# Expert weight loads of an MoE layer split by partition: 120 rows in one DMA, 8 rows in another

## The chip, the cores and the metric

The kernel runs on one core of one Trainium2 chip. The metric is the device time of one launch in microseconds (us); lower is better. A core has TensorE (matmuls), VectorE, ScalarE, GpSimd, and SyncE, which here issues nearly all DMAs, and 16 DMA engines that move the data of all of them. On-chip memory has 128 partitions.

## The reference

A trunk of two layers with 640 tokens (128 context, 512 latent) of width 1024. Each layer mixes tokens (attention and two kinds of scans), and then mixes channels by an expert-choice mixture of 16 experts. The change concerns the second half, of which this is the core:

```python
cap = EC_FACTOR * (bsz * n_tok) // N_EXPERTS
aff = jax.nn.softmax((xf @ router).astype(jnp.float32), axis=-1)
gate, idx = lax.top_k(aff.T, cap)
xe = xf[idx]
he = jax.nn.silu(jnp.einsum('ecd,edf->ecf', xe, w1)) * jnp.einsum('ecd,edf->ecf', xe, w3)
ye = jnp.einsum('ecf,efd->ecd', he, w2) * gate[..., None].astype(h.dtype)
y = jnp.zeros_like(xf).at[idx.reshape(-1)].add(ye.reshape(-1, dm))
```

Each expert takes 80 tokens (64 latent, 16 context) and has three matrices of 1024 × 1024 in float32: 12.6 MB an expert, 201 MB a layer. Everything is float32.

## The kernel before

The program is a list of phases for each of the two layers: modulation, input projection, attention, the two scans, output projection and norm, routing, experts, second norm. Each phase writes out the instruction stream of every engine by hand; order between engines is kept by semaphores, and there is no scheduler.

In the expert phase an expert is cut into four *quarters* (q = 4 x + j for expert x, quarter j). For a quarter of the hidden width, `gate(x, j)` (line 2285) runs 128 matmuls with w1 and w3 as the stationary side (64 in the source; each stands as two in the trace) and 80 tokens as the moving side; for a quarter of the output width, `project(x, j)` (line 2300) runs 64 with w2, one expert later. ScalarE applies silu (line 2390), VectorE multiplies (line 2470) and takes the projections out of PSUM (line 2430). Every two experts, TensorE turns the results (line 2311) and adds them to their tokens by a matmul with a selection matrix (lines 2329 and 2338); VectorE adds these to the residual (line 2439). GpSimd gathers the tokens of the expert after next (line 2044).

The weights come by SyncE. `load_w13` (line 2055) loads a gate quarter, 128 partitions × 4096 float32, 2 MB, into one of WG = 6 buffers; `load_w2` (line 2061) loads a projection quarter, 128 × 2048, 1 MB, into one of WP = 4. In the input each partition's row of a quarter is contiguous: 16 KB and 8 KB. Each buffer has its own semaphore (`ld_e0` to `ld_e5`, `ld_f0` to `ld_f3`), which a load raises by 16 when all of it has landed. Five gate quarters are issued in the output phase, ahead of the stores of the normalised rows to memory (line 1967); the sixth and four projection quarters in the routing phase (behind the router's weights, ahead of the context lists, line 2099). In the expert phase SyncE then goes through the quarters: it waits until gate(q) has run and loads quarter q + 6 into its buffer, waits until project(q − 4) has run and loads w2 of quarter q. The last buffers that come free take the next layer's modulation weights (line 393, five loads of 2 MB).

TensorE waits for a quarter's semaphore ahead of its first matmul (`gate_loads` gives the count), for the product of two quarters before, and within a quarter for nothing.

Of the kernel before, what the change touches and what calls it, by code (L numbers as in the profile page):

```python
# [25 lines left out]
P = 128  # L26
# [14 lines left out]
NE, FF = 16, 1024  # L41
# [1956 lines left out]


WG, WP = 6, 4  # L2000
QUARTERS = 4 * NE
FREED_GATES = QUARTERS - WG

# [5 lines left out]

def gate_loads(l, q):  # L2010

    return 16 * (l * len(range(q % WG, QUARTERS, WG)) + q // WG + 1)


def expert_memory(e):
# [36 lines left out]

def load_w13(e, sp, q, mem):

    sp.dma_start(mem["w13"][q % WG].rearrange("p a k n -> p (a k n)"), e.d["ex_w13"][e.l, q // 4, q % 4].rearrange("p a k n -> p (a k n)")
                 ).then_inc(e.S[f"ld_e{q % WG}"], 16)


def load_w2(e, sp, q, mem):

    sp.dma_start(mem["w2"][:, q % WP].rearrange("p k n -> p (k n)"), e.d["ex_w2"][e.l, q // 4, q % 4].rearrange("p k n -> p (k n)")
                 ).then_inc(e.S[f"ld_f{q % WP}"], 16)


ROUTE_SEMS = (
# [135 lines left out]
def phase_experts(e):  # L2201

    nc, d, l, S, ps, x_sb = e.nc, e.d, e.l, e.S, e.ps, e.x
    mem = expert_memory(e)
    w13, w2, xe, xT, hs, he, yS, yX, yP, yC, GP, GC, iP, gP, iC, gC, iota = (mem[k] for k in (
        "w13", "w2", "xe", "xT", "hs", "he", "yS", "yX", "yP", "yC", "GP", "GC", "iP", "gP", "iC", "gC", "iota"))
# [22 lines left out]
    with nc.Block() as block:  # L2229
        @block.sync  # L2230
        def _(sp):
# [5 lines left out]
            for q in range(QUARTERS):  # L2237
                if q + WG < QUARTERS:
                    sp.wait_ge(S["h_ps"], q + 1)
# [20 lines left out]
        def _(pe):  # L2260
# [29 lines left out]
            def project(x, j):  # L2290

                q = 4 * x + j
                pe.wait_ge(S[f"ld_f{q % WP}"], l * (16 * NE) + (x * 16 + 16))
                pe.wait_ge(S["he"], 4 * x + 4)
                if q >= 2:
                    pe.wait_ge(S["pr_sb"], q - 1)
                for b in range(2):
                    for f in range(KD):
                        for c in range(2):
                            m = nc.tensor.matmul(product(j)[c * 64:(c + 1) * 64, b, :],  # L2300
                                                 w2[:, q % WP, f, b * P + c * 64:b * P + (c + 1) * 64],
                                                 he[:, x % 2, f, :], start=f == 0, stop=f == KD - 1)
                m.then_inc(S["pr_ps"], 1)
# [297 lines left out]
```

## Time and profile before

| | us |
|---|---|
| median of 3 runs | 3454.83 (3450.43 to 3464.23) |
| the profiled execution's own time | 3457.51 |
| its span in the trace | 3455.7 |
| TensorE, matmuls busy | 2651.1 (77%) |
| TensorE, weight loads busy (beside the matmuls) | 2021.6 (58%) |
| VectorE / GpSimd / ScalarE busy | 1272.5 / 682.6 / 475.0 |
| 16 DMA engines, mean rate over the span | 154 GB/s |

How to read it: times come from one profiled execution. Engines are PE (TensorE's matmuls), PEld (its weight loads, which overlap them), DVE (VectorE), ACT (ScalarE), POOL (GpSimd), SPq (SyncE's queue). L2285 is line 2285 of the kernel. A group's idle time is that of the engine just ahead of the group's instructions, and behind the arrow stands what ended it; "issue" means that the engine waited for nothing that the profile shows. The DMA share is the mean busy share of the 16 DMA engines; the profile doesn't name the engine that a packet used. The matmuls' ends are modelled and overlap the next start. Queue q1 holds the DMAs that SyncE issues, q8 transfers of the kind "instruction". Some matmul records can be missing.

The expert phases lie at about 1105 to 1730 us and 2805 to 3427 us of the span.

### The profile page before, as it was taken

What the parts mean: (1) busy time and instruction counts of PE and PEld (TensorE: products, weight loads), DVE (VectorE), ACT (ScalarE), POOL (GpSimd) and SP (SyncE); (2) the same over time, 40 slices, a digit from 0 to 9 for tenths busy, and PEclk for the clock granted to TensorE, in tenths of its full rate; (3) what the DMA queues carried; (4) which work ended last, traced back from release to release, by engine and by line L of the source; (5) the groups of instructions that cost most, each with busy time, mean ns of one, the idle gap of its engine ahead of it and who ended that gap; (6) DMA issues with size and microseconds to landing.
All of it is one profiled execution on the core that took longest, in us unless ns stands there. A gap on an engine that the chain in (4) does not pass through costs nothing. (4 is left out here: it accounts for less than half of the span.)

```text
span 3455.7 us, 87591 instructions
## 1 busy us (share of the span) xinstructions
PE 2651.1 (77%) x40000; PEld 2021.6 (58%) x40000; DVE 1272.5 (37%) x2847; ACT 475.0 (14%) x973; POOL 682.6 (20%) x844
## 2 busy tenths in 40 slices
PE   5998883748584888888979988566585858888886
PEld 1555553638534777777725545355484457777774
DVE  1101568784523112211240026786744231112114
ACT  0102332032101000000010023302211100000001
POOL 0000908334221000000010027272430200000001
PEclk9999997869886999999999999877798879999998
DMA  8300000000053988888671010000003458888872
GB/s 350 125 25 36 1 1 11 1 7 4 3 219 139 363 339 338 308 333 325 248 301 61 4 36 1 9 3 7 2 3 123 182 188 321 344 343 335 337 287 105
DMA packets 69616, 532.75 MB, mean 154 GB/s; under 512 B 13920, under 2 KB 15776, under 8 KB 32896
## 3 DMA queue, kind: packets, MB, share of 16 engines
q1 hardware_dynamic: 66176, 516.66, 38.4%
q0 software_dynamic: 3072, 10.49, 1.1%
q8 instruction: 316, 5.18, 0.6%
q14 instruction: 52, 0.43, 0.0%
HBM read 518.34 MB, written 8.79 MB: 153 GB/s over the span
## 5 line engine op out<-in xcount | busy, mean ns | idle before, releaser
L2285 PE MATMUL ps<-arena 128*64 128x80 f32 x16384 | 620.0, 235 | 107.3 <-issue 102.6
L2285 PEld LDWEIGHTS ps<-arena 128*64 128x64 f32 x16384 | 596.0, 139 | 130.0 <-issue 128.4
L2300 PE MATMUL ps<-arena 128*64 128x80 f32 x8192 | 324.2, 234 | 55.5 <-issue 53.8
L2300 PEld LDWEIGHTS ps<-arena 128*64 128x64 f32 x8192 | 304.0, 138 | 66.0 <-issue 65.7
L526 PE MATMUL ps<-arena 128*128 128x128 f32 (+1 forms) x1088 | 296.4, 435 | 5.3 <-DVE arena L579 5.3
L2470 DVE TENSOR_TENSOR arena<-arena,ps 128x160 f32<-128x160 f32 x128 | 41.2, 322 | 653.4 <-ACT arena L2390 653.4
L526 PEld LDWEIGHTS ps<-arena 128*128 128x128 f32 x1088 | 164.8, 192 | 137.0 <-issue 131.2
L2044 POOL DMA_INDIRECT arena<-h_d,arena x32 | 39.8, 1243 | 1025.9 <-DVEq L2411 920.9
L2390 ACT ACTIVATE arena<-ps 128x160 f32<-128x160 f32 x128 | 38.8, 303 | 1132.8 <-PE ps L2285 1132.8
L583 DVE COPY arena<-ps 128x128 f32<-128x128 f32 (+3 forms) x48 | 16.3, 341 | 399.4 <-PE ps L526 287.6
L1979 PE MATMUL ps<-arena 128*128 128x512 f32 x320 | 142.9, 610 | 25.1 <-DMA arena<-in_w_out 25.1
L2430 DVE TENSOR_TENSOR arena<-ps,modc 128x128 f32<-128x128 f32 (+1 forms) x256 | 49.8, 236 | 292.1 <-PE ps L2300 292.1
L2329 PE MATMUL ps<-arena 128*128 128x512 f32 x256 | 123.4, 615 | 15.4 <-DVE x_sb L2439 12.3
L1111 PE MATMUL ps<-arena 128*128 128x256 f32 x80 | 34.9, 527 | 127.1 <-DVEq L1207 127.1
L826 POOL COPY arena<-arena 32x896 f32<-32x896 f32 x2 | 1.8, 924 | 642.1 <-DVE arena L866 642.1
L428 PE MATMUL ps<-arena,scT 128*2 128x512 f32 x384 | 88.0, 614 | 49.5 <-DMA arena<-in_ada_w 24.6
L532 PE MATMUL ps<-arena 128*128 128x512 f32 (+2 forms) x480 | 125.4, 423 | 0.0
L1979 PEld LDWEIGHTS ps<-arena 128*128 128x128 f32 x320 | 62.5, 196 | 104.6 <-issue 78.7
L532 PEld LDWEIGHTS ps<-arena 128*128 128x128 f32 x480 | 82.0, 189 | 42.8 <-issue 38.5
L883 DVE TENSOR_REDUCE arena<-ps 128x1 f32<-128x768 f32 (+1 forms) x80 | 65.8, 823 | 100.3 <-PE ps L718 93.8
L2439 DVE TENSOR_TENSOR x_sb<-x_sb,ps 128x512 f32<-128x512 f32 x116 | 78.9, 687 | 36.6 <-PE ps L2329 33.9
L1111 PEld LDWEIGHTS ps<-arena 128*128 128x128 f32 x80 | 16.0, 249 | 129.3 <-DVEq L1207 128.7
(345 smaller groups left out, 4065.3 us busy)
## 6 DMA issues: line engine op xcount, KB each, us to landing
arena<-in_ex_w SPq DMA_DIRECT2D x128, 2048.0 KB, 9.1
arena<-in_ex_w SPq DMA_DIRECT2D x128, 1024.0 KB, 9.2
arena<-in_ada_w SPq DMA_DIRECT2D x24, 2048.0 KB, 15.5
arena<-in_w_t SPq DMA_DIRECT2D x34, 512.0 KB, 3.5
arena<-in_w_out SPq DMA_DIRECT2D x4, 2048.0 KB, 10.3
arena<-in_w_tok SPq DMA_DIRECT2D x2, 3712.0 KB, 16.9
h_d<-x_sb SPq DMA_DIRECT2D x10, 512.0 KB, 2.6
arena<-in_w_uq SPq DMA_DIRECT2D x2, 1536.0 KB, 6.5
```

The lines of the kernel that those rows point to most:

```text
L428: i = nc.tensor.matmul(ps[PAIR[c], s, :], e.scT[:, k, :], slots[(2 * s + c) % RING][:, k, :], start=k == 0, stop=k == KD - 1)
L526: i = nc.tensor.matmul(ps[:, n % 8, 0:c1 - c0], ring[:, a % WRING, k, :], e.hT[:, k, c0:c1], start=k == 0, stop=k == KD - 1)
L532: i = nc.tensor.matmul(ps[:, n % 8, 0:c1 - c0], e.hT[:, k, a * P:(a + 1) * P], tokw[:, k, c0:c1], start=k == 0, stop=k == KD - 1)
L883: v.link(nc.vector.reduce_max(negm[:, i:i + 1], sc[:, 0:c1 - c0], AX))
L1111: nc.tensor.matmul(two[:, :, 0:P], kT[:, 2 * dr + g // 2, cols], qz[:, g // 2, :, cols], start=True, stop=True)
L1979: m = nc.tensor.matmul(ps[:, 2 * (t % 4) + n, :], e.mixT[:, k, t * P:(t + 1) * P], wo[:, n, k, :], start=k == 0, stop=k == KD - 1)
L2285: m = nc.tensor.matmul(gated(j)[c * 64:(c + 1) * 64, f, a, :], w13[q % WG][:, a, k, f * P + c * 64:f * P + (c + 1) * 64], xT[:, x % 2, k, ...
L2300: m = nc.tensor.matmul(product(j)[c * 64:(c + 1) * 64, b, :], w2[:, q % WP, f, b * P + c * 64:b * P + (c + 1) * 64], he[:, x % 2, f, :], s ...
L2329: nc.tensor.matmul(ps[:, 6 + h, :], GP[:, (t - 1) * P:t * P], yP[:, h * 512:(h + 1) * 512], start=True, stop=True).then_inc(S["sp_ps"], 1)
L2430: m = nc.vector.tensor_tensor(to, product(j)[:, :, c0:c1], row, ALU.mult)
L2439: m = nc.vector.tensor_tensor(x_sb[:, t, half], x_sb[:, t, half], ps[:, 6 + h, :], ALU.add)
L2470: nc.vector.tensor_tensor(he[:, b, 2 * j:2 * j + 2, :], hs[:, j % 2], gated(j)[:, :, 1, :], ALU.mult).then_inc(S["he"], 1)
```

## The change

Every load of expert weights is issued as two DMAs, for partitions 0 to 119 and for partitions 120 to 127. Both raise the semaphore of the buffer by 16, so the counts that TensorE waits for are 32 per load in place of 16. The split is such that the 120 rows go over fifteen DMA engines (8 rows each) and the 8 rows over eight engines (one each); the sixteenth engine gets no expert weights. The bytes, the buffers, the places of the loads in SyncE's stream and all other loads are as before.

```diff
+PARTS = (slice(0, 120), slice(120, P))
...
-    return 16 * (l * len(range(q % WG, QUARTERS, WG)) + q // WG + 1)
+    return 32 * (l * len(range(q % WG, QUARTERS, WG)) + q // WG + 1)
...
-    sp.dma_start(mem["w13"][q % WG].rearrange("p a k n -> p (a k n)"), e.d["ex_w13"][e.l, q // 4, q % 4].rearrange("p a k n -> p (a k n)")
-                 ).then_inc(e.S[f"ld_e{q % WG}"], 16)
+    for part in PARTS:
+        sp.dma_start(mem["w13"][q % WG][part].rearrange("p a k n -> p (a k n)"),
+                     e.d["ex_w13"][e.l, q // 4, q % 4, part].rearrange("p a k n -> p (a k n)")
+                     ).then_inc(e.S[f"ld_e{q % WG}"], 16)
...
-    sp.dma_start(mem["w2"][:, q % WP].rearrange("p k n -> p (k n)"), e.d["ex_w2"][e.l, q // 4, q % 4].rearrange("p k n -> p (k n)")
-                 ).then_inc(e.S[f"ld_f{q % WP}"], 16)
+    for part in PARTS:
+        sp.dma_start(mem["w2"][part, q % WP].rearrange("p k n -> p (k n)"),
+                     e.d["ex_w2"][e.l, q // 4, q % 4, part].rearrange("p k n -> p (k n)")
+                     ).then_inc(e.S[f"ld_f{q % WP}"], 16)
...
-                pe.wait_ge(S[f"ld_f{q % WP}"], l * (16 * NE) + (x * 16 + 16))
+                pe.wait_ge(S[f"ld_f{q % WP}"], 32 * (l * NE + x + 1))
```

SyncE's stream at the start of the expert phase, before (`ctx_d` are the context lists, `in_ex_w` the expert weights; 4096 elements are a gate quarter's row, 2048 a projection quarter's):

```order
L2236 DMA arena<-ctx_d 128x1 x4
L2055 DMA arena<-in_ex_w 128x4096 x5
L2061 DMA arena<-in_ex_w 128x2048
L2055 DMA arena<-in_ex_w 128x4096
L2061 DMA arena<-in_ex_w 128x2048
```

The same place after the change (the first two of the five gate quarters, left out the rest, and the pair of a gate and a projection quarter that repeats from there):

```order
L2241 DMA arena<-ctx_d 128x1 x4
L2057 DMA arena<-in_ex_w 120x4096
L2057 DMA arena<-in_ex_w 8x4096
...
L2065 DMA arena<-in_ex_w 120x2048
L2065 DMA arena<-in_ex_w 8x2048
L2057 DMA arena<-in_ex_w 120x4096
L2057 DMA arena<-in_ex_w 8x4096
```

Each load has become a pair, the small part right behind the large one; the order of the quarters is the same.

SyncE's stream in the output phase, before (the norm's parameters, the first expert weights, the stores of the normalised rows):

```order
L1876 DMA arena<-in_ln_g 128x1024
L1876 DMA arena<-in_ln_b 128x1024
L2055 DMA arena<-in_ex_w 128x4096 x5
L1967 DMA h_d<-x_sb 128x1024 x5
L1953 UNCONDITIONAL_BRANCH
```

And after the change:

```order
L1876 DMA arena<-in_ln_b 128x1024
L2057 DMA arena<-in_ex_w 120x4096
L2057 DMA arena<-in_ex_w 8x4096
...
L1967 DMA h_d<-x_sb 128x1024 x5
L1953 UNCONDITIONAL_BRANCH
```

Ten issues stand ahead of the five stores in place of five. TensorE's stream has the same instructions in the same order; only the counts in its waits differ.

## Rows read from the trace of the kernel before

**Rows 1.** The page: busy time by engine, and the DMA queues (packets, MB, share).
```profile
PE 2651.1 (77%) x40000; PEld 2021.6 (58%) x40000; DVE 1272.5 (37%) x2847; ACT 475.0 (14%) x973; POOL 682.6 (20%) x844
...
q1 hardware_dynamic: 66176, 516.66, 38.4%
...
q8 instruction: 316, 5.18, 0.6%
```

**Rows 2.** The line of the gate matmuls in the first layer: duration, first and last start.
```profile
L2285 PE MATMUL ps<-arena x8192: 229/233/394, 1105.2 to 1702.0; 128*64 128x80 f32 x200
```

**Rows 3.** Timeline, end of the first expert stage: start, length, engine, line, operation, count.
```profile
1727.59 1.96 PE L2338 MATMUL ps<-arena 128*128 128x512 f32 x4
```

**Rows 4.** Windows: length, busy time (count) of each engine, granted clock, DMA share, GB/s.
```profile
core 0: us, PE busy (x) PEld busy (x) DVE busy (x) ACT busy (x) POOL busy (x), PEclk, DMA share, GB/s
...
789.00:815.00 26.00, 25.56 (x834) 25.56 (x836) 11.38 (x17) 5.37 (x9) 15.78 (x13) 0.94 0.02 4
1200.00:1600.00 400.00, 337.65 (x8066) 301.19 (x8065) 78.91 (x230) 18.74 (x52) 12.77 (x10) 1.00 0.86 332
2900.00:3300.00 400.00, 341.69 (x8142) 305.76 (x8140) 79.64 (x233) 19.87 (x54) 12.85 (x10) 0.99 0.86 335
20.00:60.00 40.00, 27.63 (x110) 5.25 (x112) 4.10 (x6) 0.00 (x0) 0.00 (x0) 0.91 1.02 420
```

**Rows 5.** Waits of SyncE's queue: waited for, us in total, times, longest us.
```profile
SPq L2055 <- PE ps L2285: 739.4, 116, 15.7
...
SPq L2061 <- PE ps L2300: 381.8, 120, 14.1
```

**Rows 6.** DMA issues by line: count, KB each, median us from issue to landing.
```profile
arena<-in_ex_w SPq DMA_DIRECT2D x128, 2048.0 KB, 9.1
arena<-in_ex_w SPq DMA_DIRECT2D x128, 1024.0 KB, 9.2
...
arena<-in_w_wa SPq DMA_DIRECT2D x4, 128.0 KB, 2.7
...
arena<-in_w_g SPq DMA_DIRECT2D x2, 128.0 KB, 2.6
```

**Rows 7.** Lines of TensorE, 1200 to 1600 us: count, busy us, mean ns, idle before.
```profile
L2285 PE MATMUL ps<-arena 128*64 128x80 f32 x5248 | 196.0, 233 | 36.6 <-issue 36.6
...
L2300 PE MATMUL ps<-arena 128*64 128x80 f32 x2603 | 102.8, 233 | 19.8 <-issue 18.1 <-DVE arena L2470 1.7
```

**Rows 8.** Waits of TensorE in the first expert stage.
```profile
PE ps L2285 <- issue: 51.7, 33, 2.9
PE ps L2300 <- issue: 27.6, 26, 2.5
```

**Rows 9.** Waits of TensorE in the second expert stage.
```profile
PE ps L2285 <- issue: 50.9, 29, 3.4
PE ps L2300 <- issue: 26.2, 23, 1.9
```

**Rows 10.** Timeline of TensorE in the first expert stage; in brackets idle before, us.
```profile
1145.23 0.91 PE L2300 MATMUL ps<-arena 128*64 128x80 f32 x20 [0.82 <-issue]
1146.07 0.77 PE L2269 MATMUL ps<-ident_sb,arena 80*128 80x80 f32 x8
1146.78 3.67 PE L2285 MATMUL ps<-arena 128*64 128x80 f32 x99
1152.30 1.25 PE L2285 MATMUL ps<-arena 128*64 128x80 f32 x29 [1.85 <-issue]
1153.33 2.44 PE L2300 MATMUL ps<-arena 128*64 128x80 f32 x64
1155.54 4.86 PE L2285 MATMUL ps<-arena 128*64 128x80 f32 x127
```

**Rows 11.** Timeline of TensorE where no large transfer runs.
```profile
796.31 1.10 PE L1598 MATMUL ps<-arena 64*64 64x64 f32 x32
797.25 1.10 PE L1614 MATMUL ps<-arena 64*64 64x64 f32 x32
```

**Rows 12.** Timeline of SyncE: the first loads issued in the first expert stage.
```profile
1111.97 10.59 SPq L2055 DMA_DIRECT2D arena<-in_ex_w  x3
```

**Rows 13.** The line of the gate loads: duration of an issue (min, median, max).
```profile
L2055 SPq DMA_DIRECT2D arena<-in_ex_w x128: 327/328/1470, 958.9 to 3348.6; - x128
```

## The prediction, made before the change was run

> **What bounds the kernel now.** I read the page's totals first, then the windows by stage, then the list of waits, then the timeline of the two places that matter. TensorE is the busiest engine, 2651.1 us of 3455.7 [rows 1]. The change touches only the loads of the expert weights, so only the two expert stages count: the first of them has its first gate matmul at 1105.2 and its last, short, matmuls of the scatter at 1727.59 [rows 2, 3]. Inside, TensorE is busy 337.65 us of 400 and the DMA engines have a mean share of 0.86 at 332 GB/s; in the second layer 341.69 us, 0.86 and 335 GB/s [rows 4]. So neither is full, and the question is what the idle time of TensorE is.
>
> It is no wait for weights. SyncE, which issues the loads, waits for TensorE to free a buffer in 116 of its waits for a gate quarter, 739.4 us, and in 120 for a projection quarter, 381.8 us [rows 5]: the loads follow the matmuls. A load lands 9.1 us (gate) or 9.2 us (projection) after its issue [rows 6], and a quarter takes about 400 / 41 = 9.8 us (5248 gate matmuls in 400 us, 128 to a quarter [rows 7]), while the buffers reach six gate quarters ahead. The weights are there long before.
>
> The idle time stands under "issue": nothing that the profile shows had to end. It is 51.7 + 27.6 us in the first layer [rows 8] and 50.9 + 26.2 us in the second [rows 9], **156.4 us** in all. The timeline tells its place: from 1145.23, where one stop ends, to the beginning of the next run 20 + 8 + 99 = 127 matmuls, and that next stop, the 1.85 us before 1152.30, falls in the middle of a gate quarter (99 of its matmuls ahead of it, 29 behind), where the code has no wait at all [rows 10]. One record is probably missing, so the distance is 128 matmuls, with their 128 weight loads 256 instructions. Queue q8, kind instruction, moved 5.18 MB in 316 packets, 16 KB each, beside 80,000 TensorE instructions in the page: 253 to a packet [rows 1]. So TensorE stops where its next block of instructions should have come. At 789 to 815 us the same fetches go on, faster: 32 matmuls in 0.93 us (from 796.31 to 797.25 [rows 11]), 128 in 3.7 us, and no stop is shown there, while the DMA engines have a share of 0.02 [rows 4]. **The fetches are late only when weights use the DMA engines.**
>
> [...]
>
> **The change part by part.** (1) *A sixteenth of the weights moves from one engine to eight others.* If the fetches run on the sixteenth, they wait behind no weights. The price of one stop is then what it is at 789 to 815: none. Bounds: 0 to 156.4 us over both layers. The five loads of the next layer's modulation weights at the end of the first stage still use all engines; of the 79.3 us a few stay. Per layer TensorE could gain about 75 us.
>
> (2) *Eight engines carry 9/8 of the rows.* This is the new limit. At 20 to 60 us the engines are full: 420 GB/s at a share of 1.02, so 26.3 GB/s each, and a gate row of 16 KB takes 16.384 / 26.3 = 0.62 us, a projection row of 8 KB 0.31 us [rows 4]. An engine now has 8 of each for a quarter, 7.4 us; eight engines will have 9, 8.4 us. In the stage the share is higher than the plain rate would need (332 / 420 = 0.79, shown 0.86 less 0.01 for the fetches), a factor of 1.08, so 9.0 us a quarter. Said as a rate: the highest that the loads can reach is 332 / 0.85 × 8/9 = **347 GB/s**. From the first load's issue at 1111.97 [rows 12] until the last gate quarter can start, 58 gate quarters (2.10 MB) and 56 projection quarters (1.05 MB) have to be moved, 180 MB: 520 us, and about 9 us until the last lands. That quarter could start at about 1641. It starts now some 5 us (4.86 us for 127 matmuls [rows 10]) before its last matmul, which starts at 1702.0 [rows 2]: at 1697. So the loads allow a gain of 56 us per layer, TensorE 75. The smaller rules, and two limits so near to one another cost some us where they alternate: I take **50 us per layer, 100 in all**. Weights will be what is late next.
>
> (3) *SyncE issues twice as many DMAs*: 256 more, two more in a quarter. An issue takes 0.33 us (median 328 ns [rows 13]), 0.66 us more in 9 us during which SyncE mostly waits; hidden by its own waits of 1121 us [rows 5]. Queued behind are only the next loads, with buffers to spare. Ahead of the stage five more issues, 1.6 us, stand before the five stores of the normalised rows, and five more in the routing stage before the context lists. The stores wait for the normalisation and the lists for the top-k; nothing of it is near the end. If SyncE were late the cover would be the six quarters. I take 0, at most 3 us per layer.
>
> (4) *The counts of the waits* go from 16 to 32 a load; a load is ready when both parts are. No instruction more on TensorE: 0.
>
> Sum: 3457.5 (the profiled execution; its span is 3455.7) − 100 = 3357.5. The median of the runs shown lies 2.7 us lower, so I predict **3355 us**. The forecast's own range is 3320 (TensorE's whole gain) to 3425 (a third of it).
>
> **The rivals.** (a) *The rows of the small part get in each other's way.* Eight engines write at once to eight neighbouring partitions. No large load of the trace does that. From below: loads of 128 KB to 64 partitions land in 2.7 us, to 128 partitions in 2.6 us [rows 6], so nearly nothing. [...] From about 0.7 us a quarter on, the change is slower than before. [...] This is my rival on the other side. [...]
>
> (b) *The same happens in the large part.* [...] For it speaks only that every large load of this kernel has 128 partitions, so none shows another layout at speed; against it, again the 64-partition row.
>
> (c) *The fetches are not on the sixteenth engine.* The profile names no engine. If they are on one of the first eight, that one needs 9.0 us and 1.5 fetches of about 1.05 us a quarter (0.6% of 16 engines' span over 316 packets [rows 1]), 10.6 us: 0.8 × 58 × 2 = 93 us, **3550 us**, with the stops as before. If on one of the other seven, nothing changes: 3455. [...]
>
> (d) *Relief and load cancel*, within 0.5%: the stops go, but the eight engines give only about the rate of now, 335 GB/s instead of 347.
>
> **How the numbers follow.** Forecast 0.43; (a) 0.20; (b) 0.11; (c) on one of the first eight 0.10; (c) elsewhere with (d) 0.16. Within 0.5% (17 us) is about what a measurement of this kernel can't tell from no change. Faster: 0.43. Same: 0.16. Slower: 0.41. Cases of both signs hold most of the chance, so the range is wide: 3320 to 3570 holds the forecast, (c), (d) and the milder half of (a), and leaves out (b) and the rest of (a), 0.2.
>
> **What would show it.** Right: in the windows at 1200 to 1600 more matmuls in 400 us at a mean share above 0.86; "issue" under the lines of gate and projection down from 79.3 us to under 20 per layer; some waits of TensorE now ended by the weight DMAs; SyncE's waits for TensorE shorter. Rival (a) or (b): GB/s below 332 with landing times far over 9.1 us, and TensorE waiting for weights. Rival (c): "issue" unchanged. Wrong altogether: stages other than the two expert stages that move by more than a few us.

## The result and the profile after

The changed kernel takes **4129.73 us** (median of 4 runs, 4108.68 to 4135.49) against 3453.81 us before (median of 4, 3450.43 to 3464.23). The ratio is 1.194, its 95% interval 1.192 to 1.197: slower by a fifth, where 3355 us was forecast and the range ended at 3570. It is rival (b), that the rows of the large part get in each other's way as well. My estimate for it was 4270 us with rows at half the full rate (a quarter in 2 × 8.4 = 16.8 us) and 3860 with half of that loss; nothing of before showed a half rate. It had 0.11.

The page of the kernel after: the span, the busy times, the granted clock and the DMA share by slice, and the queues.

```profile
span 4128.7 us, 87847 instructions
...
PE 2871.1 (70%) x40000; PEld 2228.2 (54%) x40000; DVE 1272.9 (31%) x2847; ACT 475.4 (12%) x973; POOL 683.2 (17%) x844
...
PEclk8999978798689887888899998879886888878787
DMA  8200000007599999998651000000087999989983
GB/s 330 88 0 31 1 9 6 2 2 182 123 196 222 223 214 210 218 211 203 206 241 45 30 1 8 3 6 3 29 192 145 202 212 220 217 205 216 213 199 97
...
q1 hardware_dynamic: 67968, 516.67, 50.5%
...
q8 instruction: 316, 5.18, 0.6%
```

Against [rows 1] the bytes are the same (516.67 MB), and 1792 packets more carry them, but their time has gone from 38.4% of a span of 3456 to 50.5% of one of 4129: in all 1.57 times as much DMA time for the same data. Where the DMA row reads "9" in the expert stages, the engines move only 196 to 223 GB/s. VectorE, ScalarE and GpSimd are busy as long as before.

The windows say where the time went. Columns are length, busy time and count of each engine, granted clock, DMA share, GB/s. First the kernel before (up to the experts, the first expert stage), then the kernel after (the same two, then the stretches that answer to [rows 4]).

```profile
0.00:1105.00 1105.00, 791.97 (x7376) 532.42 (x7376) 493.24 (x1041) 201.12 (x396) 308.29 (x405) 0.87 0.18 68
1105.00:1730.00 625.00, 533.52 (x12624) 475.36 (x12624) 124.27 (x360) 29.93 (x82) 17.14 (x14) 0.99 0.83 319
```

```profile
0.00:1105.00 1105.00, 799.59 (x7376) 539.10 (x7376) 493.15 (x1041) 201.23 (x396) 308.80 (x405) 0.86 0.21 68
1105.00:2059.00 954.00, 631.68 (x12614) 572.79 (x12614) 120.25 (x354) 30.00 (x82) 17.03 (x14) 0.84 0.90 208
1200.00:1600.00 400.00, 262.90 (x5298) 238.62 (x5296) 50.84 (x152) 11.47 (x33) 8.93 (x7) 0.85 0.95 217
...
20.00:60.00 40.00, 29.32 (x112) 5.47 (x114) 4.10 (x6) 0.00 (x0) 0.00 (x0) 0.87 1.01 418
```

Up to 1105 us nothing has moved. The whole loss lies in the two expert stages: about 334 us in the first (the last short matmuls of the scatter start at 2062.12 in place of 1727.59 [rows 3]), 338 in the second; from that start to the first gate matmul of the second layer it is 1075 us in both kernels. The engines are *busier* than before (0.95 against 0.86) at two thirds of the rate (217 against 332 GB/s), while loads of 128 partitions at 20 to 60 us still run at 418 GB/s. So a row has become slow. Counted from the packets of SyncE's queue between 1200 and 1600 us:

```
rows of 16 KB, ns: 10% / median / 90%     of 8 KB, median
before              611 /  611 /  868          309
after               991 / 1156 / 1267          574
```

The number of rows that SyncE's queue has in flight at once tells how many engines carry them (own count, same window): 16 for 0.52 of the time before, 15 for 0.62 of it after. So the large part goes over fifteen engines, as the change says. That DMAs of 8 rows go over eight is shown by experiment 8.

What TensorE waits for in the first expert stage after (waited for, us in total, times, longest):

```profile
PE ps L2305 <- DMA arena<-in_ex_w: 165.4, 32, 9.1
PE ps L2290 <- issue: 107.3, 37, 5.8
PE ps L2305 <- issue: 41.0, 14, 4.6
```

Against [rows 8] "issue" has gone from 79.3 us to 148.3 instead of to nothing, and 165.4 us of real waits for projection weights have appeared. The last part is the clock: 98 us more of busy time for nearly the same matmuls (631.68 against 533.52), at a granted clock of 0.84 instead of 0.99. 69 + 165 + 98 = 332 of the 334 us.

Two pieces of TensorE's timeline show both kinds of waiting. Start, length, engine, line, operation, count, and in brackets the idle time before and what ended it; first from the early part of the stage, then from the late one.

```profile
1311.18 0.77 PE L2290 MATMUL ps<-arena 128*64 128x80 f32 x16 [3.04 <-issue]
1311.73 4.01 PE L2305 MATMUL ps<-arena 128*64 128x80 f32 x64
1315.42 1.99 PE L2290 MATMUL ps<-arena 128*64 128x80 f32 x47
1320.81 3.00 PE L2290 MATMUL ps<-arena 128*64 128x80 f32 x81 [3.40 <-issue]
1323.63 1.82 PE L2305 MATMUL ps<-arena 128*64 128x80 f32 x47
1328.98 1.09 PE L2305 MATMUL ps<-arena 128*64 128x80 f32 x17 [3.53 <-issue]
```

```profile
1721.68 4.18 PE L2305 MATMUL ps<-arena 128*64 128x80 f32 x64 [8.19 <-DMA arena<-in_ex_w]
1725.69 4.59 PE L2290 MATMUL ps<-arena 128*64 128x80 f32 x128
1735.56 4.08 PE L2305 MATMUL ps<-arena 128*64 128x80 f32 x64 [5.27 <-DMA arena<-in_ex_w]
...
1783.27 2.38 PE L2305 MATMUL ps<-arena 128*64 128x80 f32 x64
```

The early stops stand 16 + 64 + 47 = 127 and 81 + 47 = 128 matmuls apart, as in [rows 10], and last 3.0 to 3.5 us where they lasted 1.85 there: the fetches of instructions are still late, and later than before. The packets of queue q8 bear this out. Own count of the stops of over 0.4 us in the first stage: in the kernel before 60 of them end 1.41 us (median) behind the last landing of a 16-KB packet of q8, eight in ten between 1.29 and 1.61 us behind it; with the 120 rows alone (experiment 1) 89 end 1.46 us behind one, eight in ten 1.33 to 1.64. TensorE goes on when a block of instructions has come.

64 projection matmuls take 4.0 to 4.2 us in these lines behind stops of 3 to 8 us, and 2.38 us at 1783.27. The granted clock was 0.58 in the stretch of the first (1311.7 to 1315.7), 0.55 in that of the second (1721.7 to 1725.8) and 1.00 at 1783.3 to 1785.6. The clock record of both kernels holds only the levels 0.50 and 1.00: in the first expert stage it stands at 0.50 for 296 us of 954 after (1105 to 2059 us), and for 8 us of 625 before. So most of the time of those two lines was spent at 0.50.

### The profile page after: what moved, and what is told of

It reads as the page before. It is cut to its first block and busy times, and to the rows that moved or that the text cites. A ratio compares the mean times of both kernels' runs of the same rounds, so it can differ in the third digit from the quotient of the medians.

```text
span 4128.7 us, 87847 instructions
## 1 busy us (share of the span) xinstructions
PE 2871.1 (70%) x40000; PEld 2228.2 (54%) x40000; DVE 1272.9 (31%) x2847; ACT 475.4 (12%) x973; POOL 683.2 (17%) x844
## 3 DMA queue, kind: packets, MB, share of 16 engines
q1 hardware_dynamic: 67968, 516.67, 50.5%
## 5 line engine op out<-in xcount | busy, mean ns | idle before, releaser
L2290 PE MATMUL ps<-arena 128*64 128x80 f32 x16384 | 688.8, 249 | 219.0 <-issue 214.4
L2290 PEld LDWEIGHTS ps<-arena 128*64 128x64 f32 x16384 | 663.7, 151 | 240.7 <-issue 239.5
L2305 PE MATMUL ps<-arena 128*64 128x80 f32 x8192 | 452.4, 288 | 399.9 <-DMA arena<-in_ex_w 308.7
L2305 PEld LDWEIGHTS ps<-arena 128*64 128x64 f32 x8192 | 429.1, 184 | 419.8 <-DMA arena<-in_ex_w 320.4
L526 PEld LDWEIGHTS ps<-arena 128*128 128x128 f32 x1088 | 164.3, 191 | 135.5 <-issue 130.1
L2334 PE MATMUL ps<-arena 128*128 128x512 f32 x256 | 124.4, 619 | 15.1 <-DVE x_sb L2444 12.2
L1979 PEld LDWEIGHTS ps<-arena 128*128 128x128 f32 x320 | 62.4, 196 | 104.7 <-issue 78.6
L532 PEld LDWEIGHTS ps<-arena 128*128 128x128 f32 x480 | 82.0, 189 | 42.8 <-issue 38.5
L2578 POOL TENSOR_TENSOR x_sb<-x_sb,arena 128x1024 f32<-128x1024 f32 x6 | 16.1, 2685 | 468.9 <-ACT x_sb L2569 468.9
```

The lines of the kernel that those rows point to most:

```text
L526: i = nc.tensor.matmul(ps[:, n % 8, 0:c1 - c0], ring[:, a % WRING, k, :], e.hT[:, k, c0:c1], start=k == 0, stop=k == KD - 1)
L532: i = nc.tensor.matmul(ps[:, n % 8, 0:c1 - c0], e.hT[:, k, a * P:(a + 1) * P], tokw[:, k, c0:c1], start=k == 0, stop=k == KD - 1)
L1979: m = nc.tensor.matmul(ps[:, 2 * (t % 4) + n, :], e.mixT[:, k, t * P:(t + 1) * P], wo[:, n, k, :], start=k == 0, stop=k == KD - 1)
L2290: m = nc.tensor.matmul(gated(j)[c * 64:(c + 1) * 64, f, a, :], w13[q % WG][:, a, k, f * P + c * 64:f * P + (c + 1) * 64], xT[:, x % 2, k, ...
L2334: nc.tensor.matmul(ps[:, 6 + h, :], GP[:, (t - 1) * P:t * P], yP[:, h * 512:(h + 1) * 512], start=True, stop=True).then_inc(S["sp_ps"], 1)
```

## The experiments

Experiments 1 to 11 were run once each, 12 five times. The kernel before ran beside them on the same chip: 3452.83 us for experiments 1, 2, 3 and 5; 3439.74 for 6 to 9; 3450.92 for 4, 10 and 11; 3454.86 for 12. Its runs thus lie up to 24 us apart (3439.74 to 3464.23), and a difference of that size between single runs shows nothing. Theory A is a conjecture: rows of a load slow each other down when they are written at the same time to certain partitions, neighbours among them. Which partitions these are no run shows; where I worked out numbers from the theory, it was assumed. Rows of neighbouring partitions were slow in experiment 8 (1072 ns against 618 four apart). Its rivals are the other things that the change did: twice the DMAs, fewer engines, 9 rows on eight of them, the small part. The second question is on which engine the instruction fetches run.

**1. The large part alone.** In the stage, only rows 0 to 119 are loaded.

```diff
+    rows = P if q < WG else 120
+    sp.dma_start(mem["w13"][q % WG][:rows].rearrange("p a k n -> p (a k n)"),
+                 e.d["ex_w13"][e.l, q // 4, q % 4, :rows].rearrange("p a k n -> p (a k n)")
```

> In the expert stage each load brings the 120 rows alone, in one DMA; the 8 rows of the small part keep what the first loads left there (a sixteenth of the weights is left out). Theory A, the large part is slow because engines that write at the same time meet in the same groups of partitions: the rate stays near 210 GB/s and the time near that of the changed kernel, 4000 to 4130 us. Theory B, the eight small rows that meet in eight neighbouring partitions are the cost: the rate comes back to 310 to 340 GB/s and the time is at or below 3455 us. Theory C, two DMAs for a load are the cost: as B.

Measured 4003.69 us. The window at 1200 to 1600 us:

```profile
1200.00:1600.00 400.00, 268.01 (x5484) 244.19 (x5482) 51.28 (x154) 11.45 (x33) 8.93 (x7) 0.88 0.95 216
```

TensorE's waits from 1100 us to the end:

```profile
PE ps L2289 <- issue: 321.0, 101, 5.6
PE ps L2304 <- issue: 201.6, 61, 5.7
```

With no small part, one issue per load and 120 rows over fifteen engines (15 in flight for 0.63 of the window, own count), so 8 on each, 551 of the 677 us of loss are there; the same rate (216 against 217 GB/s) at the same share. The small part, which brings the last sixteenth of the bytes, is worth the other 126 us, and it doesn't slow the rows: their median is 1194 ns here and 1156 ns in the change. The cause is in the 120 rows.

**2. Two halves of 64 rows.** The kernel after with other parts; the rows go over 16 engines again (16 in flight for 0.63 of the window below, own count).

```diff
-PARTS = (slice(0, 120), slice(120, P))
+PARTS = (slice(0, 64), slice(64, P))
```

> Each expert load is two DMAs of 64 rows, partitions 0 to 63 and 64 to 127; all sixteen engines have the same bytes, 4 rows in each DMA. [...] Theory B (the eight rows) and theory D (one engine fewer, 9/8 of the rows on eight): about 3455 us. Theory C (two DMAs for a load): about 4130 us.

```profile
1200.00:1600.00 400.00, 266.55 (x5370) 241.86 (x5364) 51.27 (x153) 11.76 (x34) 8.93 (x7) 0.88 1.01 226
```

4047.38 us, 226 GB/s at a share of 1.01, median row 1221 ns. No engine is spared and none has more than its 8 rows, and still a row takes twice its 611 ns. So neither the missing sixteenth engine nor the 9/8 makes the loss. Twice the row time and about 4100 us was also my estimate under theory A.

**3 and 4. Two and four DMAs of all 128 rows,** each with a half or a quarter of the columns.

```diff
+    for c in range(2):
+        part = slice(c * 2048, (c + 1) * 2048)
+        sp.dma_start(mem["w13"][q % WG].rearrange("p a k n -> p (a k n)")[:, part],
+                     e.d["ex_w13"][e.l, q // 4, q % 4].rearrange("p a k n -> p (a k n)")[:, part]
+                     ).then_inc(e.S[f"ld_e{q % WG}"], 16)
```

> Each expert load is two DMAs of all 128 partitions, each with half of every row; as many DMAs and the same counts in the waits as in the changed kernel, but rows dealt to the engines as before. Theories A and B: 3455 us within 1%, perhaps a little less if shorter rows let an instruction fetch through sooner. Theory C (two DMAs for a load): about 4130 us.

> Each expert load is four DMAs of all 128 partitions with a quarter of every row, so rows are 4 KB and 2 KB. If an instruction fetch waits for whole rows ahead of it, the stops get shorter and the time falls to 3350 to 3430 us. If, as the two column halves suggest, the wait doesn't hang on the length of a row: 3460 to 3500 us, a little slower for the shorter rows and SyncE's issues.

The same window, of the kernel with two and of the one with four:

```profile
1200.00:1600.00 400.00, 340.40 (x7995) 304.40 (x7990) 78.89 (x230) 18.49 (x51) 12.77 (x10) 0.98 0.89 330
```

```profile
1200.00:1600.00 400.00, 332.15 (x7740) 295.59 (x7737) 77.33 (x224) 18.18 (x50) 12.77 (x10) 0.98 0.91 319
```

3473.18 us and 3515.22 us. Twice the issues and counts of 32 cost 20 us at most, which is within the spread of the kernel before; four times cost about 64, some 15 more than the upper end that was expected. Term (3) and (4) of the prediction were small as said. The kernel with four was meant to give a fetch a shorter row to wait for; its stops are not shorter (116.2 + 67.8 us of "issue" over both stages, 91.5 + 65.4 with two). A fetch doesn't merely wait for the one row ahead of it.

**5. No stream of weights.** In the stage each load takes 8 elements of a row in place of 4096 or 2048; TensorE computes with what lies in the buffers.

```diff
+    n = 4096 if q < WG else 8
+    sp.dma_start(mem["w13"][q % WG].rearrange("p a k n -> p (a k n)")[:, :n],
+                 e.d["ex_w13"][e.l, q // 4, q % 4].rearrange("p a k n -> p (a k n)")[:, :n]
```

> In the expert stages the loads bring 8 elements of a row in place of 4096 or 2048; the matmuls run on what the first loads left (nearly all expert weights are left out). If TensorE's stops of the kind issue are instruction fetches that wait behind weights: they fall from 156 us in both expert stages to under 15, and the time to 3455 - 150 = 3300 us, 3290 to 3320. If the stops have nothing to do with the weights: 3455 us.

The window, and TensorE's timeline in it:

```profile
1200.00:1600.00 400.00, 393.85 (x9647) 355.44 (x9648) 96.29 (x275) 22.30 (x62) 11.49 (x9) 1.00 0.06 12
```

```profile
1303.00 4.60 PE L2289 MATMUL ps<-arena 128*64 128x80 f32 x128
1307.43 2.38 PE L2304 MATMUL ps<-arena 128*64 128x80 f32 x64
1309.64 4.60 PE L2289 MATMUL ps<-arena 128*64 128x80 f32 x128
```

3259.99 us, **193 us** under before and 30 under the range expected, and no stop in these lines (1.7 us of "issue" in all under the two lines of expert matmuls). The instructions and their fetches are the same. So the reading of the profile before was right: the stops are fetches, and they are late because of the weights. They were 156.4 us under "issue"; what the other 36 us are isn't shown.

**6 and 7. Weights on few engines.** Which engines must be free for the stops to go? The gate rows are taken four apart, n of them in a DMA, so that a DMA gives one row each to n engines; the rest of the gate rows and the projection weights are left out. n goes by half stage: 8, 4, 2, 1 in the first kernel, with eight DMAs a quarter (the diff), and 15, 12, 10, 8 in the second, with four.

```diff
+SETS = ((8, 4), (2, 1))
...
+    n = SETS[e.l][q // 32]
+    for j in range(4):
+        for h in range(2):
+            part = slice(h * 64 + j, h * 64 + j + 4 * n - 3, 4)
```

> In the expert stages a gate load is eight DMAs of n rows of 16 KB, four partitions apart, one row to an engine and so on the first n engines alone: n = 8 for experts 0 to 7 and 4 for experts 8 to 15 of the first layer, 2 and 1 in the second; projection loads bring 8 elements of a row (most expert weights are left out). If TensorE's instructions come over one of the first n engines, they meet eight rows (4.9 us) per quarter there, and the stops of the kind issue stay, at half their size or more, about 10 to 40 us in such a half stage (40 us in a half stage of the kernel before); in the other parts they vanish. If they come over the sixteenth engine, as the forecast had it, no part shows a stop. The changed kernel's 14 to 15 rows in flight during a fetch speak for one of the first fifteen.

> The same with four DMAs of n rows: 15 and 12 in the halves of the first layer, 10 and 8 in the second (most expert weights are left out). Engines 9 to 16 are told apart: stops with 15 and not with 12 put the fetches on engine 13, 14 or 15, with 12 and not with 10 on 11 or 12. No stops anywhere would mean the sixteenth. If the first eight carry them, all four parts have stops.

3274.36 and 3272.53 us: hardly a stop in any half of either (4.5 and 5.4 us of "issue" over both stages), with n = 15 too. That tells nothing of the engines: the share was only 0.41 (n = 8) and 0.51 (n = 15) in the fullest halves, and 15 or more rows were in flight for only 0.17 of the time with n = 15 (1110 to 1350 us, own count), since what was left out let every queue run empty. It suggests that a fetch is late behind a *full* queue, not behind any row. The question had to be asked again with full ones (experiment 10).

**8. Eight neighbours against eight four apart.** Layer 0 loads the gate rows in eight DMAs of 8 neighbouring rows each, layer 1 in eight DMAs of 8 rows that are four apart. Both use eight engines: 8 rows are in flight for 0.70 of the first window below and more often than any other number (0.40) in the second (own count). Half of the gate rows and the projection weights are left out.

```diff
+    for j in range(4):
+        for h in range(2):
+            part = slice(h * 64 + j, h * 64 + j + 29, 4) if e.l else slice(h * 64 + 8 * j, h * 64 + 8 * j + 8)
```

> Gate loads as eight DMAs of 8 rows of 16 KB, 64 of the 128 rows; projection loads bring 8 elements of a row (the rest of the expert weights is left out). In the first layer the 8 rows are neighbours, in the second four partitions apart; engines, bytes and number of DMAs are the same. [...] Theory E (any DMA with other than 128 rows is slow, whichever partitions): both stages alike.

A window of layer 0, and one of layer 1:

```profile
1200.00:1600.00 400.00, 334.14 (x7579) 302.18 (x7580) 74.71 (x215) 17.88 (x49) 11.50 (x9) 0.92 0.52 117
...
2900.00:3200.00 300.00, 293.09 (x7122) 264.47 (x7120) 73.31 (x214) 17.27 (x47) 12.85 (x10) 1.00 0.44 143
```

TensorE's waits in the stage of layer 0:

```profile
PE ps L2296 <- issue: 63.6, 14, 9.5
PE ps L2311 <- issue: 25.2, 7, 6.2
```

3398.31 us. Between the layers only the rows that a DMA takes together differ, and rows take 1072 ns (median; a tenth over 1968) as neighbours against 618 ns four apart; the time from the first to the last gate matmul is 631 us against 507. So where eight engines write to neighbours, 89 us of "issue" come back in layer 0, 3 us in layer 1. Theory A has the right direction: rows at neighbouring partitions are the slow ones. Its size was overstated: I had put four times the row time on it, 2.4 us, and some 500 us more than without a stream; the two layers differ by 1.07 against 0.62 us a row and by 124 us. The factor of four was an assumption, and no run shows it. The rows that are neighbours in partitions are neighbours in the memory that they are read from, too, in this experiment and in all the others; so that the collision is on the side of the partitions is argued from the shape of the results, and not shown apart from the source.

**9. Full-width matmuls.** If the fetches can't be moved, fewer instructions need fewer of them. Each pair of half-width matmuls becomes one with 128 columns of weights; the weights stream as before.

```diff
-                            for c in range(2):
-                                m = nc.tensor.matmul(gated(j)[c * 64:(c + 1) * 64, f, a, :],
-                                                     w13[q % WG][:, a, k, f * P + c * 64:f * P + (c + 1) * 64],
-                                                     xT[:, x % 2, k, :], start=k == 0, stop=k == KD - 1)
+                            m = nc.tensor.matmul(gated(j)[:, f, a, :], w13[q % WG][:, a, k, f * P:(f + 1) * P],
+                                                 xT[:, x % 2, k, :], start=k == 0, stop=k == KD - 1)
```

> The kernel before with gate and projection matmuls that use all 128 columns of the array in one instruction in place of two of 64; half the instructions in these lines, all loads as before. If the stops cost by the block of instructions they fall from 113 to about half. The price is the matmul itself: transposes of this shape with 80 columns stand at 88 ns against 36 ns for a half, so a quarter needs about 96 x 88 = 8.4 us in place of 7.0. Stage times: 8.4 us and half of the stops, 0.7 us or so, against 9.5 now: 3400 to 3460 us; slower than 3500 if a full-width weight load (192 ns where 128 x 128 are loaded elsewhere) is not hidden.

TensorE's timeline, early and late in the first stage:

```profile
1305.05 13.86 PE L2284 MATMUL ps<-arena 128*128 128x80 f32 x64
...
1700.59 7.31 PE L2284 MATMUL ps<-arena 128*128 128x80 f32 x64
```

3991.64 us, over 500 us beyond the forecast of 3400 to 3460 (the expectation left more than 3500 open). The stops are gone, more than the half that was expected. But the 64 matmuls that replace 128 take 7.31 us in place of 4.60 (114 ns each against 36), and 13.86 us in the first 237 us of each stage, where the granted clock is 0.50. The stops could be had away only at a higher price.

**10. Full queues on 16, 15, 8 and 12 engines.** As experiments 6 and 7, with more rows, so that the chosen engines are really full: the four half stages have 16, 15, 8 and 12 rows to a DMA, in eight DMAs a quarter and, with 8 rows, in twelve (the other four DMAs of a quarter move 8 elements). The rest of the rows is left out, and the projection weights.

```diff
+SETS = (((16, 8), (15, 8)), ((8, 12), (12, 8)))
...
+    n, m = SETS[e.l][q // 32]
+    for i in range(12):
+        at = 64 * (i % 2) + i // 2 % 4 + 32 * (i // 8)
+        part, cols = slice(at, at + 4 * n - 3, 4), slice(0, 4088) if i < m else slice(4088, 4096)
```

> Gate loads as DMAs of n rows of 16 KB, four partitions apart, on the first n engines, enough of them that those engines are nearly always busy: experts 0 to 7 of the first layer 8 DMAs of 16 rows, experts 8 to 15 8 DMAs of 15 rows; second layer 12 of 8 rows, then 8 of 12 rows; projection loads bring 8 elements of a row (part of the expert weights is left out). With 16 rows long stops as in the changed kernel. If the instructions come over the sixteenth engine, the half with 15 rows has none; if over one of the ninth to fifteenth, the half with 15 has as many as the half with 16, and the half with 8 rows has next to none. With 12 rows: stops if it is the ninth to twelfth.

3400.18 us. One window of each half stage, in the order 16, 15, 8, 12 rows:

```profile
1150.00:1400.00 250.00, 208.36 (x4853) 189.83 (x4847) 45.77 (x140) 10.85 (x31) 8.94 (x7) 0.95 0.90 222
1450.00:1650.00 200.00, 181.39 (x4231) 160.44 (x4233) 42.99 (x121) 10.63 (x29) 5.11 (x4) 0.99 0.88 224
2850.00:3050.00 200.00, 184.65 (x4496) 167.53 (x4491) 42.89 (x129) 10.24 (x29) 7.71 (x6) 0.99 0.53 195
3100.00:3300.00 200.00, 183.12 (x4337) 163.59 (x4338) 45.62 (x130) 10.85 (x29) 5.14 (x4) 0.99 0.70 197
```

Two things come from it. First the rows: **eight** engines alone (a share of 0.53 of sixteen) move 195 GB/s, nearly what sixteen move at 0.90. The median row takes 609 ns with 8 rows to a DMA, 922 with 12, 1022 with 15 and 1044 with 16. The counts of rows in flight are those of the names: 16, 15, 8 and 12 are the most frequent ones (0.45, 0.47, 0.62 and 0.52 of their windows, own count). In steps of four, 8 rows span 32 partitions, and from the ninth on each row is 32 beyond another of its DMA. That rows get slower there may be theory A with partitions 32 apart as well as neighbours; the runs don't part that from the number of engines among rows four apart. It isn't the number of engines alone: the loads of 128 rows take 611 ns on sixteen.

Second the fetches. The profile names no engine, but while a fetch runs on an engine that is otherwise full of rows, one row fewer is in flight; on an engine without rows the number stays. Counted from the packets in the windows above and in two of the kernel after, by the fetches' numbers modulo 8. A fetch counts as clear when all the chosen engines had a row for at least half of the 0.5 us on either side of it, and one and the same count held for 70% of its own time:

```
rows to a DMA          one row fewer   as many   unclear   numbers mod 8 with "as many"
16                          21             0        18      none
15                          19             0        14      none
12                           7             5        22      5, 6, 7
8                            7            15        14      2 to 7
after, 1200-1600            35             0         7      none
after, 3250-3700            38             0         8      none
```

With 8 rows "one row fewer" has the numbers 0 and 1 alone, with 12 rows 0 to 4. The same count in layer 0 of experiment 8 (1110 to 1730 us) has 18 fetches with one row fewer, all of the numbers 0 and 1, and 47 with as many, all of 2 to 7. So the answer is not one engine: the fetches fall into at least three kinds (0 and 1, 2 to 4, 5 to 7), and come round in eights. I read that as eight engines that take turns, one for each number; that two numbers never share an engine is not shown. By that reading, and if a DMA of n rows goes over the first n engines, which no run shows by itself, two of them are among the first 8 engines, three among the 9th to 12th and three among the 13th to 15th. **None is the one without weights**: in the kernel after all eight numbers cost a row. The engine that the change set free carried no fetch.

The stops of experiment 8 say the same on their own. In its first layer eight engines were full of slow rows; of its 21 stops of over 0.4 us behind a fetch, 19 belong to fetches with the numbers 0 and 1 modulo 8, and these are 88 of 89 us. There a fetch was late when its own engine was full, and on time when it was another one. So the forecast was right that a fetch on an engine without rows is on time; it had the wrong engine, and one where there are several.

**11. Parts of 96 and 32 rows,** to put a number on theory A for another shape. Both counts go evenly over 16 engines (16 rows in flight for 0.62 of the window, own count). My estimate under theory A was 255 GB/s and 3750 to 3950 us; it rests on an assumption, which partitions slow each other, that no run shows.

```diff
-PARTS = (slice(0, 120), slice(120, P))
+PARTS = (slice(0, 96), slice(96, P))
```

> Each expert load is two DMAs, partitions 0 to 95 and 96 to 127, each over all sixteen engines (6 and 2 neighbouring rows an engine). If only DMAs of 128 rows are fast, this is as slow as the two halves of 64 or slower, 4047 us. [...]

```profile
1200.00:1600.00 400.00, 261.46 (x5219) 237.08 (x5215) 50.86 (x152) 11.47 (x33) 8.94 (x7) 0.87 1.01 218
```

4075.13 us and 218 GB/s, where theory A with its assumption had given 255. A miss: it doesn't tell these shapes apart rightly. Of the loads over 15 or 16 engines only those with all 128 partitions are fast; 120, 64 + 64 and 96 + 32 all end at 216 to 226 GB/s.

**12. A quarter of the projection weights on eight engines.** The one way left to use what was learnt: projection quarter 0 of each expert goes in 16 DMAs of 8 rows four apart, on eight engines, of which only two carry fetches by the reading in experiment 10; the others get less.

```diff
+    if q % 4 == 0 and q >= WP:
+        for i in range(16):
+            part = slice(32 * (i % 4) + i // 4, 32 * (i % 4) + i // 4 + 29, 4)
```

> The kernel before, with the first projection quarter of each expert (a twelfth of the bytes) loaded as 16 DMAs of 8 rows, four partitions apart, over the first eight engines alone, where rows kept their 0.61 us. Of the eight engines on which the instruction fetches take turns, six are above the first eight: there the weights take 11/12 of 7.4 us a quarter in place of 7.4, on the first eight 13/12. If a stop is the fetch's wait for rows on its engine, the six get a tenth or two shorter: 10 to 30 us less of 156, 3425 to 3445 us. If the first eight become the limit (8.0 us by rows, 8.6 with the usual excess, against 9.8), nothing is lost by it; SyncE's 15 more issues an expert, 5 us of 38, may delay the gate loads behind them and cost it back: 3455. [...]

3465.62 us (median of 5, 3453.35 to 3472.26) against 3454.86; ratio 1.0031 [1.0009, 1.0052]. Its window keeps the old rate, and "issue" stays at 97.6 + 59.3 us over both stages:

```profile
1200.00:1600.00 400.00, 343.94 (x8026) 308.04 (x8024) 78.89 (x230) 18.49 (x51) 12.77 (x10) 0.97 0.87 330
```

A miss, where 10 to 30 us less was expected: the same as before or a little slower. That too little was taken off the engines with the fetches is the likely reason, and is not shown. No version that loads all the weights beats the kernel before.

## Why the prediction was wrong

**What bounds the kernel: right.** The idle time is late fetches, weights make them late, and the weights themselves are early. Experiment 5 shows it: without the stream the kernel takes 193 us less, of which the rows had 156.4 as stops. Without the stream TensorE goes from one block of instructions to the next with next to no stop (1.7 us of "issue" under the two lines in experiment 5); beside it, it does not.

**(1), the fetches run on the sixteenth engine: failed.** The prediction had no row for it, and gave it 0.43 as the forecast against 0.26 for its rival (c). Experiment 10 shows several engines in turn, none of them the one without weights. The whole gain of the forecast rested on this step. Taking that engine out can't give anything, whatever the rows do: the stops stayed, 148.3 us in place of 79.3 in the first stage. That a fetch on an engine without rows is on time was right (experiment 8: of 89 us of stops, 88 belong to the fetches on the full engines).

**(2), the new rate limit: failed, and this is the loss.** 26.3 GB/s an engine and 0.62 us a row were taken from loads of 128 partitions and carried over to 120. The row time hangs on the shape of the load: 0.61 us with 128 rows, 1.16 us here. The limit was not 347 GB/s but hardly more than the 217 measured, since the fifteen engines had 14.6 rows in flight in the mean between 1200 and 1600 us (own count). Rival (b) had this step; its price, 16.8 us a quarter with rows of the large part at half rate, was an estimate with no run behind the half. The rows came out at 1.9 times their old length rather than twice, 1.16 and 0.57 us: 8 of each are 13.8 us, 9 of each 15.6, and a quarter takes 14.5 over the stage ((2030.9 − 1105.1) / 64) and 15.1 in its middle, from the 12th to the 48th. What spoke against it was a bad witness. A load of 128 KB to 64 partitions lands in 2.7 us [rows 6], but that is 2 KB a row, four rows to an engine. Rows of 2 KB take 84 ns (median in the second kernel of experiments 3 and 4), so all four are 0.3 of the 2.7 us, and twice that would hardly have stood out. I read the row as evidence for large loads, and experiment 2 is exactly that case at size: 64 partitions, and 226 GB/s where 420 is full.

Why a row of these loads is slow is not shown. What the runs have is this: 226 GB/s with two halves of 64 rows between 1200 and 1600 us, and 217 to 218 in other windows of the stages (experiment 2), 216 with the 120 rows alone (experiment 1), 218 with 96 and 32 (experiment 11), beside 332 for loads of 128 rows on demand and 420 at full. Three ways to cut by partitions end near one rate, and no run shows how the rows of a load are dealt to the engines.

**The 9/8 of (2), and rival (a).** The small part costs 126 us (experiment 1), and rows don't get slower by it. A quarter goes from 13.5 to 14.5 us, 7% more, and the bytes do the same (128 rows for 120), at a rate of 217 against 216 GB/s. So the runs show neither the 9/8 of the eight engines, which would be 12.5%, nor that the eight small rows get in each other's way. The range of the prediction took in the milder half of rival (a), with prices of 3525 us in the middle and 3685 at the worst that I worked out from rows at a quarter of their rate; no run shows a quarter, and eight neighbours at a time took 1.07 us a row against 0.62 (experiment 8). Of the places of the 8 rows the runs show the number, eight engines (8 in flight in experiment 8), and not which.

**Why TensorE waits for fetches although weights are the limit.** Own count of when a gate quarter's rows have all landed and when TensorE starts it, us:

```
quarter            12                30                48
before       1161.9 / 1201.4   1335.4 / 1381.0   1509.3 / 1555.2
after        1208.1 / 1255.4   1475.9 / 1527.4   1750.4 / 1800.3
120 alone    1192.3 / 1247.2   1450.7 / 1514.2   1707.5 / 1767.7
```

Gate weights are still 40 to 60 us early. With the 120 rows alone TensorE waits only 0.9 us for expert weights; it loses 522.6 us to fetches (321.0 + 201.6, experiment 1), three times as much as before. The windows and the packets fit together: the queues, which before had a share of 0.86, are now full nearly always (14.6 rows in flight on fifteen engines), and a fetch on an engine full of rows of 1.2 us comes late nearly each time (89 stops of over 0.4 us behind a fetch in the first stage of experiment 1, of 98 fetches; a fetch's own packet takes 1.31 us in the median where it took 0.98). The late fetches then hold TensorE back to about the pace of the loads, which have next to nothing to spare: in the middle of the stage, quarters 12 to 48 above, a quarter takes 14.5 us. That weights would be late if the fetches were not is argued from this, not shown. In the whole change the projection weights, which have four buffers to the gate's six, come late as well in the second half of a stage.

**(3) and (4): right** within what single runs tell: at most 20 us by experiment 3, in which twice as many issues stand in SyncE's stream.

**The clock had no term.** TensorE's granted clock fell from 0.99 to 0.84 in the first expert stage and from 0.98 to 0.83 in the second, and its busy time grew by 98 and 111 us. The stretches at a low clock that the timelines show (0.58 and 0.55) stand behind stops of 3 to 8 us. If the stops bring them on, slow loads cost a second time; that is my reading, and experiment 9 has the clock at 0.50 without any stop.

**The chances.** (b) had 0.11 and lay outside the range. The argument against it was one landing time of small loads; with no row of a large load of another shape, both layouts should have stood near even, and the range should have reached them.

## What to carry to other kernels

Here a load's rate depended on how it was cut by partitions: 16-KB rows took 0.61 us (median) in loads of 128 partitions, and 1.16 to 1.22 us in parts of 120 and 8, 120 alone, 64 and 64, and 96 and 32 (own counts). Before cutting a 128-partition load by partitions, time loads of the new shape at full size and one behind the other, since a small one shows next to nothing of what a row costs (four rows of 84 ns in a landing of 2.7 us here). If rows must go on fewer engines, eight rows four partitions apart to a DMA kept their speed (0.61 to 0.62 us on eight engines). And stops of TensorE every 128 matmuls (256 instructions) beside full DMA queues were instruction fetches here: 156 us of them went to 1.7 us without the stream (experiment 5), and a fetch was on time when its own engine was free (experiment 8); leaving one engine free of weights helped nothing here, since it carried no fetch.

## What the runs showed of the hardware that was not expected

- Instruction fetches take turns over several DMA engines, in an order that comes round every eight fetches (experiment 10; eight engines by my reading): two of the eight places are on the eight engines that a DMA of 8 rows uses, five on the twelve of one of 12 rows, all eight on the fifteen that carry the 120 rows. In experiment 8 88 of 89 us of stops belong to the two places on the full engines.
- With the weights streaming, late fetches cost 156 us of stops of 3455 here; with a share of up to 0.51 in experiment 7 next to nothing (5.4 us of "issue"), but at 0.52 on eight engines with slow rows 89 us in one layer (experiment 8). Rows of a half or a quarter of the length don't help (156.9 and 184.0 us of "issue").
- Loads of 120, 64 + 64 and 96 + 32 rows of 16 KB run at 216 to 226 GB/s over 15 or 16 engines; loads of 128 rows at 330 on demand and 420 at full. Eight engines with rows four partitions apart move 195 GB/s alone. Which partitions slow each other stays open: neighbours do (1072 ns against 618), beyond 8 rows four apart they got slower (922 to 1044 ns against 609), and my numbers for theory A missed for eight neighbours (2.4 us) and for 96 and 32 rows (255 GB/s).
- A matmul with 64 columns of float32 weights and 80 columns moving takes 36 ns in a row of its kind, one with 128 columns 114 ns: two halves (72 ns) are faster than one whole here.
- The granted clock is no constant of a stage. With full-width matmuls and no stops at all it stayed at 0.50 for the first 237 us of the stage (64 matmuls in 13.86 us) and then rose to 1.00 (7.31 us).
